# Attention units spread over six pairs of groups, and another spread of the convolution taps, in a one-core encoder layer

## The reference, cut to what matters

```python
proj = x @ w_in                                   # q (8 heads), k, v (2 kv heads), u (2 x 512)
attn = window_attention(rotary(q), rotary(k), v)  # chunks of 64 see their own and the previous chunk, with sinks
c = silu(layer_norm(dwconv31(u1 * sigmoid(u2))))  # 31 taps, 512 channels
h = layer_norm(ALPHA * x + concat(attn, c) @ w_out)
up = h @ w_up                                     # 2 x 2816 columns
f = (silu(dwconv3(up)[..., :2816]) * dwconv3(up)[..., 2816:]) @ w_down
y = layer_norm(ALPHA * h + f + sigmoid(h @ w_pg + b_pg) * (p @ w_pe))
```

## Time and profile before

| | |
|---|---|
| median of 3 runs | 2532.84 us (2531.83 to 2533.19) |
| the profiled execution | 2529.42 us |
| its span, first to last instruction | 2527.6 us |
| PE busy | 2374.0 us, 94% |
| POOL, DVE, ACT busy | 63%, 58%, 50% |
| mean granted TensorE clock | 0.970 |
| share of the chain that ended last: PE, DVE, ACT | 83%, 8%, 4% |

### The profile page before, as it was taken

The page is one execution under the profiler, slowest core; times in us unless marked ns, Lnnn a source line. Parts: engine busy times, 40 slices in busy tenths (PEclk is TensorE's granted clock), DMA queues, the critical chain, the costliest instruction groups (busy, mean ns, idle before and its releaser), DMA issues.

```text
span 2527.6 us, 38650 instructions
## 1 busy us (share of the span) xinstructions
PE 2374.0 (94%) x15013; PEld 2335.3 (92%) x15013; DVE 1470.6 (58%) x2366; ACT 1276.4 (50%) x2060; POOL 1599.9 (63%) x1284
## 2 busy tenths in 40 slices
PE   7578999899999999999999999999999999979995
PEld 7478999899999989999998999999999999979995
DVE  5835886366676447666644666663566665354433
ACT  4336656455553535645353564445465445456653
POOL 8246787765566667556566655656675665757873
PEclk9789999999999999999999999999999999989998
DMA  6133454544333454333344433334443333525442
GB/s 231 67 102 112 154 176 147 182 129 138 116 120 123 132 166 142 115 117 126 124 143 149 150 114 115 121 119 155 144 159 117 117 126 111 172 96 181 162 148 88
DMA packets 119046, 341.54 MB, mean 135 GB/s; under 512 B 15312, under 2 KB 43600, under 8 KB 118864
## 3 DMA queue, kind: packets, MB, share of 16 engines
q1 hardware_dynamic: 93360, 308.70, 37.2%
q10 hardware_dynamic: 25504, 30.37, 3.7%
HBM read 330.12 MB, written 8.99 MB: 134 GB/s over the span
## 4 chain that ended last, share of the span: by engine, by line
PE 83%; DVE 8%; ACT 4%; issue 2%; POOL 2%; DMA 1%; ACTq 0%; DVEq 0%
PE ps L483 27%; PE ps L485 26%; PE ps L484 26%; DVE sq L1059 2%; POOL w_lo L434 2%; DVE res L999 1%; PE ps L550 1%; PE ps L522 1%; ACT w_hi L577 1%; DMA w_raw<-in_panels 1%; DVE acc L999 1%; PE ps L531 1%; PE ps L541 1%; ACT sq L770 1%; DVE a_lo L871 1%
## 5 line engine op out<-in xcount | busy, mean ns | idle before, releaser
L434 POOL TENSOR_TENSOR w_lo<-w_raw,w_hi 128x512 fp32r<-128x512 f32 (+1 forms) x1272 | 1598.9, 1283 | 891.5 <-ACT w_hi L577 890.2
L577 ACT CAST w_hi<-w_raw 128x1024 fp32r<-128x1024 f32 (+1 forms) x636 | 622.8, 982 | 586.3 <-PE ps L485 447.4
L483 PE MATMUL ps<-h_hi,w_hi 128*128 128x386 f32 (+5 forms) x2496 | 819.4, 328 | 19.5 <-issue 15.9
L484 PE MATMUL ps<-h_lo,w_hi 128*128 128x386 f32 (+5 forms) x2496 | 810.0, 325 | 0.0
L485 PE MATMUL ps<-h_hi,w_lo 128*128 128x386 f32 (+5 forms) x2496 | 809.7, 324 | 0.0
L483 PEld LDWEIGHTS ps<-h_hi,w_hi 128*128 128x128 f32 x2496 | 476.3, 191 | 27.8 <-issue 22.7
L484 PEld LDWEIGHTS ps<-h_lo,w_hi 128*128 128x128 f32 x2496 | 477.0, 191 | 1.8 <-issue 0.6
L485 PEld LDWEIGHTS ps<-h_hi,w_lo 128*128 128x128 f32 x2496 | 476.9, 191 | 0.0
L483 PE MATMUL ps<-f_hi,w_hi 128*128 128x384 f32 (+2 forms) x1264 | 414.8, 328 | 5.5 <-POOL w_lo L434 2.8
L484 PE MATMUL ps<-f_lo,w_hi 128*128 128x384 f32 (+2 forms) x1264 | 408.0, 323 | 0.0
L485 PE MATMUL ps<-f_hi,w_lo 128*128 128x384 f32 (+2 forms) x1264 | 407.7, 323 | 0.0
(11 more groups left out here) (118 smaller groups left out, 2001.4 us busy)
## 6 DMA issues: line engine op xcount, KB each, us to landing
w_raw<-in_panels SPq DMA_DIRECT2D x540, 512.0 KB, 3.3
w_raw<-in_panels SPq DMA_DIRECT2D x48, 384.0 KB, 3.0
w_raw<-in_panels SPq DMA_DIRECT2D x48, 128.0 KB, 2.3
xres<-in_xT ACTq DMA_DIRECT2D x32, 192.0 KB, 3.0
out_yT<-res ACTq DMA_DIRECT2D x4, 1536.0 KB, 5.7
a_raw<-in_xT ACTq DMA_DIRECT2D x6, 768.0 KB, 6.6
out_yT<-res ACTq DMA_DIRECT2D x2, 1024.0 KB, 5.0
x_raw<-in_xT ACTq DMA_DIRECT2D x1, 1536.0 KB, 10.2
```

The lines of the kernel that those rows point to most:

```text
L434: ins = pool.tensor_tensor(w_lo[:, n % WS, c], w_raw[:, n % RS, c], w_hi[:, n % WS, c].bitcast(F32), ALU.subtract)
L483: pe.matmul(out, w_hi[:, sl, c], hi, start=k == 0, stop=False)
L484: pe.matmul(out, w_hi[:, sl, c], lo, start=False, stop=False)
L577: act.copy(w_hi[:, n % WS, 0:w], w_raw[:, n % RS, 0:w]).then_inc(w_hi_done, 1)
```

## The change

The attention steps of a unit stand at pairs +0, +2, +4 and +5 of six, in place of +0, +1, +2 and +3 of four; so the three units take pairs 1 to 18 in place of 1 to 12, and `att_split` stands behind pair 20 in place of 14. The taps are counted out over pairs 0 to 25 in place of 0 to 24. The ten steps of `cln` all stand one pair later. No instruction of arithmetic is added or taken away. The added text is three lines shorter, so line numbers below the table are 3 lower in the changed kernel (L1059 becomes L1056).

```diff
-            for n, name in enumerate(("scores", "divide", "turn", "mixed")):
-                if k == 1 + 4 * u + n:
+            for n, name in ((0, "scores"), (2, "divide"), (4, "turn"), (5, "mixed")):
+                if k == 1 + 6 * u + n:
                     stage(name, t, u)
-        if k == 5 + 4 * (UNITS[t] - 1) + 1:
+        if k == 2 + 6 * UNITS[t]:
             stage("att_split", t)
...
-        taps.update({n: (2, 4) for n in range(13, 21)})
...
+        taps = dict(enumerate([(0, n) for n in (4, 4, 4, 4, 4, 3, 3, 3, 3)] + [(1, n) for n in (7, 7, 7, 7, 4)]
+                              + [(2, n) for n in (4, 5, 5, 5, 5, 4, 4)] + [(3, n) for n in (7, 7, 7, 7, 4)]))
...
-        if k in (7, 12, 20):
-            stage("conv_in", t, {7: 1, 12: 2, 20: 3}[k])
-        for name, n in (("tree", 25), ("mean", 26), ("centre", 26), ("square", 27), ("sqtree", 28), ("var", 29),
-                        ("root", 29), ("scale", 30), ("affine", 31), ("lo", 32)):
+        if k in (8, 13, 20):
+            stage("conv_in", t, {8: 1, 13: 2, 20: 3}[k])
+        for name, n in (("tree", 26), ("mean", 27), ("centre", 27), ("square", 28), ("sqtree", 29), ("var", 30),
+                        ("root", 30), ("scale", 31), ("affine", 32), ("lo", 33)):
```

More of the change, by code:

```diff
@@ L79, in mix_at @@
         for u in range(UNITS[t]):
-            for n, name in enumerate(("scores", "divide", "turn", "mixed")):
-                if k == 1 + 4 * u + n:
+            for n, name in ((0, "scores"), (2, "divide"), (4, "turn"), (5, "mixed")):
+                if k == 1 + 6 * u + n:
                     stage(name, t, u)
-        if k == 5 + 4 * (UNITS[t] - 1) + 1:
+        if k == 2 + 6 * UNITS[t]:
             stage("att_split", t)
-        taps = {8: (1, 4)}
-        taps.update({n: (0, 4) for n in range(8)})
-        taps.update({n: (1, 7) for n in range(9, 13)})
-        taps.update({n: (2, 4) for n in range(13, 21)})
-        taps.update({n: (3, 8) for n in range(21, 25)})
+        taps = dict(enumerate([(0, n) for n in (4, 4, 4, 4, 4, 3, 3, 3, 3)] + [(1, n) for n in (7, 7, 7, 7, 4)]
+                              + [(2, n) for n in (4, 5, 5, 5, 5, 4, 4)] + [(3, n) for n in (7, 7, 7, 7, 4)]))
         if k in taps:
             stage("taps", t, *taps[k])
-        if k in (7, 12, 20):
-            stage("conv_in", t, {7: 1, 12: 2, 20: 3}[k])
-        for name, n in (("tree", 25), ("mean", 26), ("centre", 26), ("square", 27), ("sqtree", 28), ("var", 29),
-                        ("root", 29), ("scale", 30), ("affine", 31), ("lo", 32)):
+        if k in (8, 13, 20):
+            stage("conv_in", t, {8: 1, 13: 2, 20: 3}[k])
+        for name, n in (("tree", 26), ("mean", 27), ("centre", 27), ("square", 28), ("sqtree", 29), ("var", 30),
+                        ("root", 30), ("scale", 31), ("affine", 32), ("lo", 33)):
             if k == n:
```

## The result

| | before | changed |
|---|---|---|
| median | 2532.76 us (2527.79 to 2535.11, 16 runs) | 2539.16 us (2536.37 to 2543.54, 16 runs) |
| ratio | | 1.0026, 95% interval 1.0019 to 1.0034 |
| profiled execution | 2529.42 us, span 2527.6 us | 2537.2 us, span 2535.4 us |

The change makes the kernel 6.4 us slower, which a measurement of this kernel tells from no change. The forecast was +3.2 us, 2536.0; the measured difference is twice that, and its interval, 4.8 to 8.6 us by the ratio, leaves +3.2 out. The sign was forecast, and "slower" had been given 0.36, less than "same" with 0.47.

The account below looks back on a forecast made before the run. TensorE was taken as the bound, without idle time in tiles 1 to 4 and with 11.84 us in tile 0. Tile 0's -0.3 and tiles 1 to 4's +3.5 gave +3.2, 2536.0 us; range 2526.5 to 2544.5.

Parts of the forecast that it names:

- (a): Tile 0, turns: both waits for the divided probabilities go, -3.7 us, with the clock's fall behind them, -1.8 us.
- (b): Tile 0, block 7: the second unit's exponentials hold ScalarE, so d part 0 waits for f_lo, +2.3 us.
- (c): Tile 0, pairs 13 to 20: the third unit's work delays VectorE's block 15, lengthening PE's wait by +1.2 us.
- (d): Tile 0, mean: the tree moves behind pair 26, where the input's split precedes it; new wait of +2.0 us.
- (e): Tile 0, variance: the squares' tree waits for pair 29's product and PE has less work meanwhile; +1.9 us.
- (f): Tile 0, pairs 30 to 37: waits for weight panels behind the affine shrink, -5.6 us, bounds -8.6 and +1.3.
- (g): Tile 0, clock: two falls behind new or remaining waits, +3.4 us, between 0 and 6.8.
- Tiles 1 to 4: Stretches after tile 0: waits at d (+1.0 us) and for the variance (+2.5 us), together +3.5 us.
- the first: Rival: tile 0's new waits stay hidden and the clock holds; -7.6 us, 2525 us, chance 0.17.
- The second: Rival: ScalarE decides tile 0's pairs 30 to 37, panels gain nothing, clock falls at every wait; +13.5, 2546 us, chance 0.20.
- The third: Rival: PE still waits at turns because probabilities come late by more than a pair; 2541.5 us, chance 0.03.

Follow-up runs that it names:

- w3_turn_half_later: The kernel before with only turn and mixed of tile 1's first two units half a pair later; 2533.73 us, ratio 1.0005.
- c_before_again: The kernel before, unchanged, measured and profiled a second time as a control; 2533.32 us, ratio 0.9997.
- e6_scores_after_8: The changed kernel with the second unit's scores behind pair 8 in place of 7; 2536.40 us, ratio 1.0016 of before.
- the second execution: The repeat profile of an unchanged kernel, before or changed as the sentence concerns; medians on repeating 2533.32 us (before) and 2538.97 us (changed).
- e2_norm_later: The kernel before with only the ten steps of cln one pair later; 2542.27 us, ratio 1.0037.
- e5_affine_later: The kernel before with only scale, affine and lo of cln one pair later (31, 32, 33); 2532.60 us, ratio 0.9994.
- e4_taps: The kernel before with only the new table of taps and the new places of conv_in; 2537.29 us, ratio 1.0018.
- w4_best: Changed kernel with second unit's scores behind pair 8, norm at its old pairs, last block's taps eight each in pairs 21 to 24; 2530.24 us.

## Why the prediction was right, and where it was not

The sign and the mechanism in tiles 1 to 4 were right. In tile 0 the sum came out right by luck, with two terms wrong that cancelled, and only in the first of two executions. By the median the size was missed by half, and not all of that is found in the stretches.

(a) The turn waits went, 3.7 us. But the forecast treated them as a gain of their own; w3_turn_half_later shows that they pay for block 7. It is the work moved out of pairs 0 to 8 that makes them worth something. The clock lost there, priced at 1.8, was no gain of its own either, as c_before_again shows. From the start of the stretch to the first `d` group the changed kernel takes 64.46 us in place of 68.95; about 2.0 of these 4.5 are PE's own work moved on (tile 1 shows it), which leaves 2.5 for (a) and (b) together, forecast at 3.2. What I left out: `mixed` waits 1.30 and 1.87 us for the copies.

(b) Block 7: +2.3 forecast, 2.43 and, again, 2.44 measured; 0.2 to 0.3 in tiles 1 to 4, where the idle time is 0.12 and e6_scores_after_8, which takes it away, shortens the stretch by 0.34. Right as to the wait. But this place was not free of waits before: 0.33 us, and 1.85 in the second execution.

(c) Pairs 13 to 20: 54.15 - 49.28 = 4.87 us longer. Tiles 1 to 3, without a wait in these pairs, are 3.79 longer, which is PE's own work moved there (3.6 forecast). So +1.1, forecast +1.2. It shows as the wait of `mixed` at 342.44, not as a wait of `d` part 1.

(d) The mean: +2.0 forecast, 3.00 and, again, 2.62 measured. That the tree ends at 400.12, as forecast, is chance, since pair 25 starts at 379.71 us here and started at 380.75 before. Counted from that start, PE came at 17.5 us as forecast (17.4), and the tree ended at 20.4, not 19.4:

```profile
396.56 2.03 DVE L1056 TENSOR_TENSOR sq<-a_raw 128x768 f32<-128x768 f32 x1
398.62 1.50 DVE L1056 TENSOR_TENSOR sq<-sq 128x384 f32<-128x384 f32 x1
```

The tree took 3.56 us. I had taken the 2.85 of the squares' tree for it, in which the same first add takes 1.28 and not 2.03.

(e) The variance: 1.74 us of wait in tile 0 for 1.9 forecast, 0.48 in tiles 1 to 3 for 0.7; the stretch of e2_norm_later, which has no other wait there, is 0.75 longer.

(f) The panels: this step failed, and by its mechanism. Forecast -5.6 us in pairs 30 to 37 with (e) apart. From its first `pg` group on, this part took 37.03 us before and 36.45 after, and 37.74 in the second execution; with the 1.7 of (e) in it that is -0.6 or +0.7, so (f) with its clock was -2.3 or -1.0. I had gone through the order by hand and found that the panels behind the affine would have more cover. e5_affine_later shows that they have none: the first wait is what ScalarE's block without a cast, 6.6 us, leaves after the casts ahead of it, and a pair later that is no less.

(g) The clock: forecast +3.4 us for two more falls. They did not come in the first execution: none of the waits of (b) to (e) brought one, the fall behind the wait of block 15 went too, and the clock was 0.98 over the stretch against 0.96. In the second, the waits of (b) and (d) brought one each, and it was 0.97. Whether a wait of 1.7 to 3.0 us brings a fall is not fixed by the order. This took the place of the gain that (f) did not bring, which is why tile 0 came out at -0.5 and +2.5 where -0.3 was forecast.

Tiles 1 to 4: +3.5 forecast, 4.2 and 4.3 measured.

Of the rivals, the first (b to e hidden) did not come: each wait is on the timeline. The second, that ScalarE decides pairs 30 to 37 so that (f) wins nothing, was right in that the later affine wins nothing, but its mechanism is not needed for that: e5_affine_later has no additional table load and no later square root, and wins nothing either. The rival's clock falls and its 1.3 us did not add up to 13.5 us. The third did not come.

What is left: the median says +6.4 us (4.8 to 8.6), the stretches +3.7 and +6.8 in two executions. Outside the stretches nothing is changed, yet their rest (span less the five stretches) is 1056.8 and 1058.4 us in the two profiles of before, and 1059.2 to 1065.3 in the twelve others. A part of it is the clock: between the second and the third stretch it stood at half for 3.4 us in both profiles of before, and for 6.8 in all twelve others. The two of before were themselves 2 to 3 us below the median of their kernel, and the medians of e5_affine_later and w3_turn_half_later do not show such a rest. Whether a changed kernel moves its start and its clock falls outside, or whether these were two quick executions, the runs do not settle. The 4.8 us of e4_taps belong to this.

## What to carry to other kernels

A wait at one place may be the bill for a stage that ends further on: before removing it, ask whether the engine that is waited for has less to do, and if not, expect the wait at the next place where its results are needed. In an order written by hand, what must not stand ahead of a join (here a `d` part behind block 7, a mean behind the last tap) is every instruction of the in-order engines that feed it, and the copy that waits for another engine above all. Shifting a block that starves a queue moves the wait; only making it shorter took some of it away.

## What was not expected of the hardware

The add of 128x2048 on VectorE took 2.5 to 3.4 us in thirteen traces and 6.26 us in one, by how it met GpSimd's subtractions. The Trainium skill ("SBUF — State Buffer", SBUF: two separate sides) says that the two engines share a port pair as an exclusive lock for a whole instruction, so that the loser fully blocks. The rows agree: in w4_best, where the add had its turn after one subtraction, GpSimd's next one took 3.34 us in place of 1.29. But they show more: in e6_scores_after_8 the add, begun at 299.78, waited for the running GpSimd instruction and for three more that began after it (four in 5.00 us from 298.89), and got its turn only when GpSimd had nothing to do. That it is this lock which held the add is read from the rows and the page; no run changes only that. A latency of 2.5 us in a plan can so be 6.3.
